# Eight of the merge gate's 24 weight chunks are computed in the first projection stage instead of the stick-breaking stage

## What is computed

```
z = RMSNorm(x) @ w_in          # 7424 columns = 58 chunks of 128
  A: q, k, v, gate             # sliding-window attention with sinks
  B: q, k, v, gate             # stick-breaking attention, 8 heads of 64
  C: q, gate                   # attention to a memory of 256 rows
  m: 3 x 1024 merge gates      # the last 24 chunks
y_i = (o_i * silu(g_i)) @ w_br_i
x + (sum_i sigmoid(m_i) * y_i) @ w_out, then RMSNorm
```

## Time and profile before

| | |
|---|---|
| median of 3 runs | 3097.01 us (3094.26 to 3100.07) |
| the profiled execution | 3091.68 us |
| its span, first to last instruction | 3090.0 us |
| granted TensorE clock, mean | 0.975 |
| PE busy | 2896.4 us, 94% |
| VectorE, ScalarE, GpSimd busy | 49%, 33%, 37% |
| DMA | 485.98 MB, mean 157 GB/s |

### The profile page before, as it was taken

The page is one execution under the profiler, slowest core; times in us unless marked ns, Lnnn a source line. Parts: engine busy times, 40 slices in busy tenths (PEclk is TensorE's granted clock), DMA queues, the critical chain, the costliest instruction groups (busy, mean ns, idle before and its releaser), DMA issues. The chain is left out here.

```text
span 3090.0 us, 50524 instructions
## 1 busy us (share of the span) xinstructions
PE 2896.4 (94%) x20331; PEld 2384.9 (77%) x20331; DVE 1513.3 (49%) x2135; ACT 1004.6 (33%) x1843; POOL 1147.8 (37%) x1001
## 2 busy tenths in 40 slices
PE   6899999999989999989998999899988996999798
PEld 5788888888877888867776777677766776877686
DVE  7232221100004777666766676567657774333333
ACT  6441211111113444434443444334435662000221
POOL 4242331111104445445544545345535563433100
PEclk9899999999999999999999999999998998999899
DMA  6543332212216554665466545754448348444443
GB/s 215 178 154 114 131 123 68 79 68 71 73 66 215 171 162 156 223 214 176 159 215 217 185 159 175 240 189 159 150 153 229 126 128 238 165 169 163 163 143 109
DMA packets 383015, 485.98 MB, mean 157 GB/s; under 512 B 27888, under 2 KB 241904, under 8 KB 382416
## 3 DMA queue, kind: packets, MB, share of 16 engines
q1 hardware_dynamic: 341200, 359.32, 36.9%
q0 software_dynamic: 34688, 111.05, 9.6%
q10 hardware_dynamic: 6912, 12.59, 1.2%
HBM read 359.28 MB, written 123.60 MB: 156 GB/s over the span
## 5 line engine op out<-in xcount | busy, mean ns | idle before, releaser
L376 PE MATMUL prj_bank<-hidden_hi,w_hi 128*128 128x512 f32 (+2 forms) x1360 | 490.9, 361 | 13.1 <-DVE w_lo L439 13.1
L378 PE MATMUL prj_bank<-hidden_hi,w_lo 128*128 128x512 f32 (+2 forms) x1360 | 487.1, 358 | 0.0
L377 PE MATMUL prj_bank<-hidden_lo,w_hi 128*128 128x512 f32 (+2 forms) x1360 | 486.8, 358 | 0.0
L1100 POOL TENSOR_TENSOR stk_beta<-stk_beta,stk_left 128x1024 f32<-128x1024 f32 (+4 forms) x160 | 275.8, 1724 | 549.2 <-DVE stk_left L1017 549.2
L809 PE MATMUL stk_g_bank<-hidden_hi,w_hi 128*128 128x512 f32 (+2 forms) x928 | 351.1, 378 | 14.6 <-PEq L62 10.8
L811 PE MATMUL stk_g_bank<-hidden_hi,w_lo 128*128 128x512 f32 (+2 forms) x928 | 336.6, 363 | 0.0
L810 PE MATMUL stk_g_bank<-hidden_lo,w_hi 128*128 128x512 f32 (+2 forms) x928 | 335.8, 362 | 0.0
L376 PEld LDWEIGHTS prj_bank<-hidden_hi,w_hi 128*128 128x128 f32 x1360 | 256.9, 189 | 44.8 <-DVE w_lo L439 13.3
L378 PEld LDWEIGHTS prj_bank<-hidden_hi,w_lo 128*128 128x128 f32 x1360 | 256.7, 189 | 32.5
L377 PEld LDWEIGHTS prj_bank<-hidden_lo,w_hi 128*128 128x128 f32 x1360 | 257.0, 189 | 31.3
L1017 DVE TENSOR_TENSOR_SCAN stk_left<-stk_rest,stk_left 128x513 f32<-128x513 f32 x192 | 244.6, 1314 | 8.1 <-ACT stk_rest L965 8.0
(11 more groups left out here) (254 smaller groups left out, 5460.2 us busy)
## 6 DMA issues: line engine op xcount, KB each, us to landing
stk_kd<-in_cache_sb_k SPq DMA_DIRECT2D x64, 1024.0 KB, 5.4
stk_vd<-in_cache_sb_v SPq DMA_DIRECT2D x64, 1024.0 KB, 7.3
w_raw<-in_w_in SPq DMA_DIRECT2D x112, 512.0 KB, 3.8
scratch_zT<-stk_g_out POOLq DMA_DIRECT2D x72, 256.0 KB, 2.3
mrg_gate<-scratch_zT SPq DMA_DIRECT2D x24, 768.0 KB, 4.4
scratch_zT<-prj_z POOLq DMA_DIRECT2D x48, 256.0 KB, 2.3
prj_w<-in_w_in SPq DMA_DIRECT2D x18, 512.0 KB, 3.9
mrg_u_raw<-scratch_uT SPq DMA_DIRECT2D x9, 1024.0 KB, 9.2
```

Of the source, the lines that this page charges most:

```text
L376: pe.matmul(out, w_hi[u][:, k, :], hi[:, k, :], start=k == 0, stop=False)
L377: pe.matmul(out, w_hi[u][:, k, :], lo[:, k, :], start=False, stop=False)
L378: last = pe.matmul(out, w_lo[u][:, k, :], hi[:, k, :], start=False, stop=k == KC - 1)
L1100: pool.tensor_tensor(bt, bt, left[prompts.index(n) % 2][:, :, 1:keys + 1], ALU.mult).then_inc(a_done, 1)
```

## The change

Eight merge-gate chunks (34 to 41 of `w_in`) join the list of the projection stage, behind all others, emptied with Sigmoid. `GL` is the first chunk that stays in the stick stage; 16 are left there, and `shares` spreads their 80 pieces (74 behind the lead) over the same slots. The loads that are made ahead, the addresses of weights and of stores follow `GL`.

```diff
@@ -45,6 +45,7 @@
 QA, KA, VA, GA, QB, KB, VB, GB, QC, GC, GM = 0, 4, 5, 6, 10, 14, 18, 22, 26, 30, 34
+GL = GM + 8
@@ -287,7 +288,8 @@
-              + [(c, "copy") for c in range(QC, QC + 4)] + [(c, "silu") for g in (GA, GB, GC) for c in range(g, g + 4)])
+              + [(c, "copy") for c in range(QC, QC + 4)] + [(c, "silu") for g in (GA, GB, GC) for c in range(g, g + 4)]
+              + [(c, "sigmoid") for c in range(GM, GL)])
@@ -295,7 +297,7 @@
-    plain = [n for n in range(N * G) if kind[n] in ("copy", "silu") or (n in splits and n % G == G - 1)]
+    plain = [n for n in range(N * G) if kind[n] in ("copy", "silu", "sigmoid") or (n in splits and n % G == G - 1)]
@@ -348,7 +350,7 @@
-            for i, c in enumerate([c for c, _ in chunks] + [GM, GM + 1, GM + 2]):
+            for i, c in enumerate([c for c, _ in chunks] + [GL, GL + 1, GL + 2]):
@@ -426,7 +428,7 @@
-                act.activation(z[n % Z][:, 0:width], src[:, 0:width], ACT.Silu if kind[n] == "silu" else ACT.Copy).then_inc(emptied, 1)
+                act.activation(z[n % Z][:, 0:width], src[:, 0:width], {"silu": ACT.Silu, "sigmoid": ACT.Sigmoid}.get(kind[n], ACT.Copy)).then_inc(emptied, 1)
@@ -585,7 +587,7 @@
-    GC_N = 24
+    GC_N = GM + 24 - GL
@@ -736,7 +738,7 @@
-                c = GM + x % GC_N
+                c = GL + x % GC_N
@@ -1078,7 +1080,7 @@
-                pool.dma_start(d["zT"][GM + c, :, tokens(p)], g_out[:, 0:w]).then_inc(g_stored, 16)
+                pool.dma_start(d["zT"][GL + c, :, tokens(p)], g_out[:, 0:w]).then_inc(g_stored, 16)
```

## The result

The kernel after takes 3118.33 us (3117.44 to 3125.2, 4 runs) beside 3097.83 us (3094.26 to 3100.07, 4 runs) before: a ratio of 1.0078, 95% interval 1.0064 to 1.0093. That is +24.2 us on 3097.01; the two medians themselves lie 20.5 us apart. The forecast was 3109 us, +12, with 3098 to 3122 as its own range and 3092 to 3132 over all cases: slower, as forecast, and some twice as much as forecast, at the upper edge of its own range. The profiled execution took 3118.03 us with a span of 3116.4 us. The profiled one of before was a quick one, 5.3 us under its median, so the two spans differ by 26.4 us, a few us more than the medians do.

The account below looks back on a forecast made before the run. PE's own work was taken to set the pace in both stages, so moving chunks is first neutral. Terms -5 + 5 + 12.4 = +12.4 us gave 3104.1 for the profiled execution, 3109 us as a median; range 3092 to 3132 us.

Parts of the forecast that it names:

- Projection: Projection stage: eight chunks more at 23.40 us each, +187.2 us, all but the matmuls lying under PE.
- Pieces: Stick stage: 40 pieces less, -194.2 us; with the projection's +187.2 between 0 and -7.0, taken as -5.
- Weights, roundings, remainders, stores: Stick stage: 32 weight loads, 32 roundings, 32 GpSimd remainders and 40 stores gone; nothing directly.
- Start: Start of the stick stage: the first free piece comes a slot later, uncovering a wait for ScalarE; +5 us.
- Runs and key slots: Stick-stage slots without a piece: two more bad key slots, +6.4, ten more long runs, +6; +12.4, from +6.4 to +29.4.
- Token-group changes: Three changes of token group in the stick stage: PE's waits follow ScalarE's order and stay; zero, from -3 to +3.
- Merge: Behind the stick stage: the merge reads the same gates from the same memory; zero.
- the rival with VectorE: Stick stage: VectorE becomes the bound, long and short runs without a piece cost more; +34 us, 3131 us, chance 0.14.
- no change: Stick stage: VectorE's backlog fits in the slack nearly everywhere, only the start costs; +2 us, 3099 us, chance 0.23.
- the clock: Stick stage: each of twelve new waits costs 2.5 us of PE's clock on top; +42 us, 3139 us, chance 0.05.
- Faster through GpSimd: Stick stage: fewer GpSimd remainders relieve VectorE, taking 15 us off PE's waits; -18 us, 3079 us, chance 0.11.
- the 75 us: Sign against the forecast: PE's waits in the stick stage passing 75 us, from 50 before.

Follow-up runs that it names:

- doubled remainders: The kernel after, with GpSimd working out every second weight remainder twice (31 more, 80 us in all): 3170.2 us, ratio 1.0235 to the kernel before.
- the kernel with covered key slots: The kernel after, with the planner's threshold lowered so that only three of six prompt-unit key slots have no piece: 3120.69 us, 1.0078.

## Why the forecast was right in sign and half the size

1. *Projection, +187.2: right.* +187.7, rounding still every 23.40 us, nothing else waited. A missing item: the barrier behind this stage, +0 in the forecast, measured -6.3. It is shown to come with the projection's program, as GpSimd's DRAIN of 6.92 or 0.72 us; what sets its length is open.

2. *Pieces, -194.2, with the projection -5, from 0 to -7: the step that failed most.* The stage's busy time fell by 182.8, 22.9 us a chunk, so the two together are +4.9, outside my bounds. I set the lower bound at the projection's 23.40 us, and no row forbade less. What failed is how much of the entry cost I let stay, 2 us of 194.2. Taken from start to start in both traces, without the waits, the pieces' own matmuls gave 196.5 us less, close to my reading of the earlier trace rows. But the units' matmuls, the same in number, took 13.7 us more. The largest part, 7.6 us, is the step from the transposes of the sigmoid products to the next scores: it takes 0.205 us, 108 times before and 144 times after, where the step from them into a piece takes 0.036 us. The clock has a small share in it: length times (1 - granted clock) over windows of some 20 us adds up to 26.4 us in before and 27.8 in after.

3. *Weights, roundings, remainders, stores: nothing. Right only where cover is full.* With a third of the remainders gone from before and all else kept the time is the same. With 74 pieces the same third is worth some 50 us. The forecast priced the thinner cover by rows of before, where GpSimd carried all its remainders, and took the relief as nothing. PE's idle time rose by 25.6 us with the relief and by 56 with the doubled remainders (107.4 beside 51.1); terms 4 and 5 said 17.4. So the cover was priced far too low and the relief left out, and that the two errors stand against each other is luck.

4. *Start, +5: right in kind, too low.* The waits for ScalarE there went from 2.8 + 3.3 to 12.0, +5.9, and slot 7 adds a wait of 2.97 for VectorE. Without their pieces the slots 0 to 12 took 39.1 us before and 45.5 after. It is the noisiest place of the kernel, with its DMA engines full, but the other kernels tell: with before's start it took 39.1, 41.4 and 43.4 us in three of them, with after's 45.5, 49.1, 53.8 and 54.2 in four, some 9 us more on the mean. The profiled execution of after had a good start.

5. *Runs and key slots, +12.4 with bounds of 6.4 and 29.4: within.* Key copies rose to 28.2 us in all instead of 17.5 (+10.7; I gave +6.4, and slot 7 is 3 of the difference), sums and products by 6.3 (I gave 6). My count was off: long runs go from 8 to 20, which is twelve more and not ten. And the waits listed per slot aren't a price that can be bought back: covering three of the bad slots took 5.6 us of waits away and gave 2 us.

6. *Token-group changes, zero: right.* 3.9 + 4.3 + 7.0 = 15.2 us of ScalarE's waits became 5.21 and two more of the same line, 28.1 - 12.0 = 16.1.

7. *Merge, zero: +2.0 behind the stage,* within what one execution tells from another.

Missed: the wait for the value block in the tail, +3.3 (6.0 us in what lies behind slot 231), shown by laying a piece over it.

The range: the upper bounds of my terms add up to +38 (0 + 6 + 29.4 + 3) and not to the +25 that I gave as the forecast's own; the rest I had left to the rival with VectorE.

Over the forecast by 13.8 us in the profiled executions: +0.5 projection, -6.3 barrier, +9.4 pieces (-182.8 for -192.2), +8.2 idle time (25.6 for 17.4), +2.0 behind. The rivals: no change falls (1.0064 at least), the clock falls (27.8 beside 26.4 us, where it wanted 29.5 more). Faster through GpSimd falls by the result; its mechanism is real in the kernel after, as term 3 says, and was smaller than the loss of cover. VectorE as the bound is the nearest. PE's waits went past the 75 us that I had set as the point where my forecast is wrong (76.7 with the value load and ScalarE in it), so by its own sign the forecast just fails. Yet only 10.7 + 6.3 - 1.5 = 15.5 of the 25.6 us more are VectorE's, and the rows behind long runs are the 6 us forecast and not 23. It takes hold with sixteen chunks moved.

## What to carry to other kernels

Work that fills another engine's waits has two prices: its own time, which moves with it, and the cover, which doesn't; here eight chunks moved 187 us and left PE idle 25.6 us longer. Don't price cover by the count of pieces: the profiled executions lose 31, 30 and 122 us for four, eight and sixteen chunks. Two single places, the start and the tail, cost their share from the first four on, and the middle gave way with the last eight. Waits listed per slot tell where cover is missing, but a wait bought off in one slot comes back in the slots that paid for it. A change that takes cover away and relieves an engine at the same time needs both measured apart and together: here each alone told little of the two. And list, before a forecast, all that sits in the stretch around a moved step: the barrier, the transfers of the start, and the last piece's place in the tail made 6 to 9 us each here.

## What had not been expected of the hardware

- PE's gap at the barrier between two stages depends on the program ahead of it: 10.8 and 10.7 us with 34 chunks in the projection, 12.4 with 38, 4.5 or 4.6 with 42 (eight kernels), 8.1 with 50. The chunk count of that stage is what sets these groups apart, and the difference is the length of one DRAIN on GpSimd (6.92, 8.56, 0.72 and 3.98 us for 34, 38, 42 and 50); what sets that is open.
- GpSimd's work cost nothing in one kernel and much in the other: 32 remainders fewer took 26 us off VectorE and nothing off the time of before; 31 more (80 us on GpSimd) in the kernel with 74 pieces added 46 us to VectorE's busy time and some 50 us to the kernel. Of VectorE's instructions the scans changed in both, the gate product in before alone, and the copies out of PSUM in neither.
- Idle time of PE and time lost to the clock rise together, in no fixed proportion. The same sum over windows is 26.4 us with 51 us idle (before), 27.8 with 77 (after), 49.5 with 107 (doubled remainders); from the clock's records it is 36 us with 79 us idle (the kernel with covered key slots) and 57 with 138 (sixteen chunks moved). The change itself costs 1.4 us of it.
